# State space scan: where the products with the sines are made

## The reference, cut to what matters

```python
u = h @ w_in
a_re = mag * jnp.cos(lam_im * dt); a_im = mag * jnp.sin(lam_im * dt)    # mag = exp(lam_re * dt)
bu_re = jnp.einsum('sbgk,gpk->sbgp', ut, bb_re)                          # 64 groups of 16 inputs, 64 states
bu_im = jnp.einsum('sbgk,gpk->sbgp', ut, bb_im)
_, _, xr, xi = lax.associative_scan(combine, (ar_t, ai_t, bu_re, bu_im), axis=0)   # x_t = a x_(t-1) + bu_t, complex
y = jnp.einsum('sbgp,gkp->bsgk', xr, c_re) - jnp.einsum('sbgp,gkp->bsgk', xi, c_im)
y = jax.nn.gelu(y.reshape(B, S, D_MODEL) + d_skip * u)
y = y * jax.nn.sigmoid(y @ w_glu)
return y @ w_o
```

## Time and profile before

| | |
|---|---|
| median of 3 runs | 3458.79 us (3454.75 to 3462.83) |
| the profiled execution | 3465.3 us, span 3463.2 us |
| mean granted clock of TensorE | 0.945 of full speed |
| busy, share of the span | PE 91%, DVE 50%, ACT 33%, POOL 8% |
| the loop over the 32 blocks | first L2277 at 590.29 us, last L2296 at 723.91 us |

### The profile page before, as it was taken

One profiled execution on the slowest core, in us unless ns is written; L12 is line 12 of the kernel. 1 busy time (PEld: TensorE's weight loads), 2 busy tenths in 40 slices (PEclk: granted clock), 3 DMA queues, 4 the chain that ended last, 5 costly groups with the idle time before them and its releaser, 6 DMA issues.

```text
span 3463.2 us, 41926 instructions
## 1 busy us (share of the span) xinstructions
PE 3151.0 (91%) x16692; PEld 2659.9 (77%) x16693; DVE 1721.9 (50%) x2275; ACT 1127.1 (33%) x1163; POOL 276.2 (8%) x227
## 2 busy tenths in 40 slices
PE   4988998887999999999998999987899999799998
PEld 3857887366777777777866998875689989686898
DVE  6434433936778777873003541566345255232553
ACT  1121031005667666663002431111134244123442
POOL 0008201930000000000000000003100000000000
PEclk9959999998999999999999999986899999899999
DMA  7714775025899889996542654430046446540462
GB/s 233 252 43 147 245 253 157 1 73 170 293 337 314 285 295 329 308 303 214 160 166 77 195 157 146 146 121 0 30 141 211 149 130 197 143 146 25 147 206 76
DMA packets 578779, 607.90 MB, mean 176 GB/s; under 512 B 37385, under 2 KB 533100, under 8 KB 578668
## 3 DMA queue, kind: packets, MB, share of 16 engines
q1 hardware_dynamic: 565255, 602.50, 53.7%
q10 hardware_dynamic: 13413, 3.81, 0.7%
HBM read 605.22 MB, written 1.05 MB: 175 GB/s over the span
## 4 chain that ended last, share of the span: by engine, by line
PE 79%; DVE 8%; DMA 6%; issue 3%; ACT 2%; SPq 1%; ACTq 1%; POOL 0%; DVEq 0%; POOLq 0%
PE bank L900 22%; PE bank L801 22%; PE bank L827 4%; PE bank L1177 3%; PE bank L1170 2%; PE bank L1206 2%; PE bank L1207 2%; PE bank L1174 2%; PE bank L1154 2%; PE bank L1211 2%; DMA ring<-in_o_exp_up 2%; DMA ring<-in_o_exp_down 2%; PE bank L1324 2%; PE bank L813 2%; DVE std L2285 1%
## 5 line engine op out<-in xcount | busy, mean ns | idle before, releaser
L2028 DVE TENSOR_TENSOR ring_r<-ring,store_area_r 128x2048 fp32r<-128x2048 f32 (+1 forms) x274 | 644.8, 2382 | 117.6 <-ACT store_area_r L1472 114.4
L801 PE MATMUL bank<-hT,ring 128*128 128x256 f32 x2624 | 582.0, 384 | 30.7 <-DVE hT L1920 23.5
L1472 ACT ACTIVATE store_area_r<-ring 128x2048 fp32r<-128x2048 f32 (+1 forms) x274 | 535.7, 1984 | 155.0 <-PE bank L900 79.2
L801 PEld LDWEIGHTS bank<-hT,ring 128*128 128x128 f32 x2624 | 504.5, 193 | 102.5 <-issue 32.6
L900 PE MATMUL bank<-sq_r,store_area_r 128*128 128x256 f32 x1408 | 207.4, 291 | 21.0 <-ACT sq_r L1508 21.0
L900 PEld LDWEIGHTS bank<-sq_r,store_area_r 128*128 128x128 f32 x1408 | 188.1, 196 | 25.3 <-issue 22.5
L900 PE MATMUL bank<-sq_r,ring_r 128*128 128x256 f32 x1408 | 200.8, 286 | 0.0
L900 PE MATMUL bank<-hT_r,store_area_r 128*128 128x256 f32 x1408 | 200.0, 285 | 0.0
L2375 DVE TENSOR_TENSOR ring_r<-ring,store_area_r 128x3072 fp32r<-128x3072 f32 (+1 forms) x56 | 170.7, 3089 | 58.3 <-ACT store_area_r L1751 58.2
L1519 ACT ACTIVATE silu_g<-bank 128x512 f32<-128x512 f32 x55 | 32.9, 597 | 467.7 <-PE bank L900 300.6
L900 PEld LDWEIGHTS bank<-sq_r,ring_r 128*128 128x128 f32 x1408 | 184.8, 195 | 0.0
(11 more groups left out here) (404 smaller groups left out, 4597.2 us busy)
## 6 DMA issues: line engine op xcount, KB each, us to landing
ring<-in_o_exp_gate SPq DMA_DIRECT2D x88, 1024.0 KB, 6.4
ring<-in_o_exp_up SPq DMA_DIRECT2D x88, 1024.0 KB, 8.9
ring<-in_ffn_w_gu SPq DMA_DIRECT2D x88, 1024.0 KB, 7.5
ring<-in_o_exp_down SPq DMA_DIRECT2D x32, 1536.0 KB, 8.1
ring<-in_ffn_w_down SPq DMA_DIRECT2D x32, 1408.0 KB, 9.1
ring<-in_o_exp_down SPq DMA_DIRECT2D x32, 1280.0 KB, 10.9
ring<-in_ssd_w_in SPq DMA_DIRECT2D x32, 1024.0 KB, 6.9
ring<-in_e_mod_mix_w SPq DMA_DIRECT2D x12, 1024.0 KB, 11.4
```

The source lines that it names most:

```text
L801: i = mm(banks[2 * u.r + s][:, t * T:(t + 1) * T], w[:, k, t * P:(t + 1) * P], rhs(k), start=(k == 0), stop=(k == kk - 1))
L1472: activation(dst, slot(u, s, kk), ACT.Copy).then_inc(w_high, 1)
L2028: nc.vector.tensor_tensor(slot(u, s, kk, rounded=True), slot(u, s, kk), as_f(high), ALU.subtract).then_inc(w_low, 1)
```

## The change

The sine products leave GpSimd. One VectorE operation of 1024 columns now writes cosine and sine products of a block, [cosines, sines] of `s5_table` times the scanned parts, the latter repeated by a broadcast, into `s5_u[j % 2]`, which lies in the same memory as `s5_u1` and `s5_u2` did. The semaphore `w_ready` and the waits on it (GpSimd's signal, one wait of VectorE ahead of the scans, one of TensorE ahead of its third product) are gone; GpSimd keeps the two adds.

```diff
-    s5_u1 = [rs[:, 2 * T * n:2 * T * (n + 1)].rearrange("p (c t) -> p c t", c=2) for n in range(2)]
-    s5_u2 = [act[:, 16 + 2 * n:18 + 2 * n, :] for n in range(2)]
+    s5_u = [t.rearrange("p (n c t) -> p n c t", n=2, c=2) for t in (rs, flat2(act[:, 16:20, :]))]
...
-                for i in range(NS + 1):
-                    if i < NS:
...
-                    if i >= 1:
-                        j = i - 1
-                        pool.wait_ge(scanned, j + 1)
-                        if j >= 2:
-                            pool.wait_ge(w_used, j - 1)
-                        nc.gpsimd.tensor_tensor(s5_u2[j % 2], s5_z[j % 2], s5_sin_t[:, j:j + 1, :].to_broadcast([P, 2, T]), ALU.mult)\
-                            .then_inc(w_ready, 1)
+                for i in range(NS):
+                    pool.wait_ge(bu_turned, i + 1)
+                    t = s5_t[i % 2]
+                    nc.gpsimd.tensor_tensor(t[:, 0, 0, :], t[:, 0, 0, :], t[:, 1, 1, :], ALU.add)
+                    nc.gpsimd.tensor_tensor(t[:, 0, 1, :], t[:, 0, 1, :], t[:, 1, 0, :], ALU.subtract).then_inc(turned, 1)
...
-                        y, u1, u2 = banks[3 + m % 3][part, 0:T], s5_u1[j % 2], s5_u2[j % 2]
+                        y, u1, u2 = banks[3 + m % 3][part, 0:T], s5_u[j % 2][:, 0, :, :], s5_u[j % 2][:, 1, :, :]
...
-                        pe.wait_ge(w_ready, j + 1)
...
-                        if j >= 2:
-                            ve.wait_ge(w_ready, j - 1)
...
-                        nc.vector.tensor_tensor(s5_u1[j % 2], s5_z[j % 2], s5_cos[:, j:j + 1, :].to_broadcast([P, 2, T]), ALU.mult)\
-                            .then_inc(back_c, 1)
+                        z = s5_z[j % 2].rearrange("p (n c) t -> p n c t", n=1)
+                        nc.vector.tensor_tensor(s5_u[j % 2], z.to_broadcast([P, 2, 2, T]),
+                                                s5_table[:, :, j:j + 1, :].to_broadcast([P, 2, 2, T]), ALU.mult).then_inc(back_c, 1)
```

## The result

| | time, us | runs |
|---|---|---|
| before | 3458.13 | 3454.75 to 3463.05, 6 runs |
| changed | 3473.53 | 3468.71 to 3479.02, 6 runs |

The ratio is 1.0041, with a 95% interval from 1.0029 to 1.0052: 15.4 us, between 10 and 18. The forecast was 3476.

What follows compares the result with a forecast made beforehand. VectorE was taken to set the scan's pace at 3.865 us a group. Product 17.1, start -1.5, end -1.1 and -0.3, clock +3.5 gave +17.7 on 3458.8, told as 3476 us; range 3465 to 3490.

Steps and rivals of the forecast that it cites:

- L741 frees nothing on DVE's path (0): Scan loop, middle: removing GpSimd's 32 sine products of 1.72 us saves VectorE 0, as the adds are released by L2277.
- The product grows by 0.534 us, the group to 4.40: Cosine product L2291, 512 to 1024 columns: +0.534 us, group 3.865 to 4.40 us, 17.1 us over 32 products.
- The adds go on blocking: Scan pair and product: GpSimd's two adds still cost VectorE 0.9 us a group; the rival that they stop had 0.07.
- The start covers -1.5: Start of the scan stage: VectorE's idle time waiting for TensorE at half clock absorbs 1.5 us (0 to 3.2) over six groups.
- The end gives -1.4 (-1.1 and -0.3): End of the stage: last scan pair without GpSimd work beside it, -1.1 us; last four output matmuls in one piece, -0.3.
- The clock: two to three additional stretches at 1.3 to 2.1 us, +3.5: Scan loop: TensorE, idle more per group, falls to half clock two to three more times, +3.5 us (0 to +28).
- PE late for most of the stage (0.20): Rival, scan loop: TensorE at half clock needs 5.49 us a group for half the stage or more, 3487 to 3501; chance 0.20.
- Nothing behind the stage takes it back: After the scan stage: all later work moves by the same amount, so the total grows by the loop's +17.7 us.

## Why the prediction was right, point by point

- *L741 frees nothing on DVE's path (0).* Right in the middle, and shown alone: without it and without a substitute the group stays at 3.87.
- *The product grows by 0.534 us, the group to 4.40.* Right: 49.4 - 32.3 = 17.1 us over 32 products, undisturbed groups of 4.40, product 1.56 to 1.57. Without the adds it takes 1.225 us, where L2302 took 1.226, so the repeated operand costs nothing extra. With the clock at 1.00 in both kernels the loops differ by 16.2.
- *The adds go on blocking.* Right: 1.74, 1.03 and 1.10 are unchanged. Their price was put at 0.9 us a group; taken away they gave 0.83. The rule cited from the Trainium skill ("SBUF — State Buffer", section "Who interferes with whom") is borne out: the same scan pair takes 1.74 us beside the adds and 1.26 without them, and a product out of PSUM 1.21 to 1.22 beside GpSimd's work or not.
- *The start covers -1.5.* The six groups that it counted, the second to the seventh, took 29.28 us after 28.19, +1.09 where six products add 3.20: it covered 2.1, and 2.5 if the 0.38 by which group six exceeds 4.40, counted below under the clock, is taken out. So this term was too small by 0.6 to 1.0.
- *The end gives -1.4 (-1.1 and -0.3).* Right. From the last turn product to the last skip operation it is 8.94 us after 9.19, -0.25; with the two doubled products there (2 x 0.53) that is -1.3. The last scan pair, beside no GpSimd work, takes 1.26 us instead of 2.33:

```profile
733.54 1.26 DVE L2272 TENSOR_TENSOR_SCAN std<-s5c,silu_g 128x256 f32<-128x256 f32 x2
...
734.84 1.23 DVE L2279 TENSOR_TENSOR act<-std,store_area 128x1024 f32<-128x1024 f32 x1
...
738.07 0.48 DVE L2284 SCALAR_TENSOR_TENSOR act<-act,vc,bank 128x256 f32<-128x256 f32 x1 [2.01 <-PE bank L1094]
```

- *The clock: two to three additional stretches at 1.3 to 2.1 us, +3.5.* The sum came out, its factors did not: nine additional stretches, ten behind the start, in which the groups from the sixth on exceed 4.40 (4.79) by 3.2 us in all, 0.32 a stretch. The count was a guess from two events. The price of one was worked out from the 5.49 us that PE needs for a group at half clock, with only some of it taken off for slack; but at 4.40 us a group PE enters the stretch with room, and by the groups' times most stretches end before much of it is used up. The kernel without the sine products shows the other side: at 3.87 us a group six such stretches cost 6.7 us, 1.1 each. That too many stretches and too dear a stretch met at 3.5 is luck. The forecast does not hang on it: start and clock together were put at +2.0, and came to +0.7 by the groups (-2.5 and +3.2), or +0.4 by the kernels with fillers. The whole loop by these terms is 17.1 - 2.5 - 1.3 + 3.2 = 16.5, where 16.6 was read.
- *PE late for most of the stage (0.20).* The first half came, 65 of 150 us at half clock, the second did not. Of the rivals it was the nearest.
- *Nothing behind the stage takes it back.* Not contradicted: loop +16.6 in one execution, +15.4 in the medians; the loop's start alone lies anywhere from 582.92 to 594.14 us in the executions profiled, so the difference says nothing. The stretch from the loop's end to the end of the span is 2739.3 us before and 2735.1 now, but it lies anywhere from 2728.9 to 2739.3 in the ten kernels profiled, so that one execution of each can't settle it.

## What to carry to other kernels

Before moving work from GpSimd to VectorE, look beside what it runs. GpSimd's work next to a VectorE operation that reads PSUM was free here, and the same engine's adds, next to scans and products with two SBUF operands, cost VectorE 0.8 us a group, more than doing them itself (0.66). So the work to take over was the adds and not the larger product; and a product moved onto the engine that sets the pace costs its full columns, merged or not.

## What the runs showed of the hardware that was not expected

Two filler loops, 8 matmuls before the first block and 1 or 2 before each further one, were worth 4.0 us (kernel before) and 4.4 us (changed) in the loop by the traces, and 5.2 and 3.1 us in the medians. Behind the first output products, ahead of which PE had stood idle for 6.5 us, TensorE's clock went on falling though PE was idle for less than 2 us at a time (1.82 ahead of the output products at 659.56 in the changed kernel). It fell seven times at an unchanged group of 3.87 us when only the wait in the middle of TensorE's work was gone. Neither the length of the group nor the one piece decides it alone, as the kernel without the adds shows: its four output products run in one piece as well, and the clock falls twice, at the start and near the end. What goes with the number of falls is PE's wait ahead of the output products:

```profile
659.56 0.62 PE L1091 MATMUL bank<-store_area 128*32 128x256 f32 x2 [1.82 <-DVE store_area L2279]
```

```profile
663.62 0.62 PE L1091 MATMUL bank<-store_area 128*32 128x256 f32 x2 [1.28 <-DVE store_area L2278]
```

```profile
665.35 0.62 PE L1086 MATMUL bank<-act,store_area 128*32 128x256 f32 x2 [0.60 <-DVE act L2272]
```

These are the changed kernel, the one without the sine products and the one without the adds. All kernels without fillers, each by one execution, with the wait of a group at full clock:

| kernel | group, us | wait ahead of the output products, us | stretches at 0.50 in the loop |
|---|---|---|---|
| adds on VectorE, sine product on GpSimd | 3.71 | 0.47 | 2 |
| without the adds | 3.57 | 0.60 | 2 |
| before | 3.87 | 0.63 to 0.72 | 2 |
| without the sine products | 3.87 | 1.28 | 7 |
| product split | 4.47 | 1.50 | 11 |
| all on VectorE | 4.25 | 1.52 | 10 |
| changed | 4.40 | 1.82 | 11 |

No run varies this wait by itself, so that it is the cause is not shown.

How long the clock is down says little of its price: behind the third group, 61 us at half clock cost nothing where the first half of the product was signalled early (split product, group 4.47), and 31 us cost 6.7 us where DVE's group was 3.87. The likely reason, that the shorter group leaves TensorE less room, was not tested by itself.
